# Attention scores as one fp32r product over a stack of high and low parts, in place of an fp32 product over 64 rows

## The chip, the cores and the metric

One core of one Trainium2 chip runs the whole block. The metric is the device time in microseconds of one execution. Engines: PE (TensorE, matmuls; its weight loads are listed as PEld), DVE (VectorE), ACT (ScalarE), POOL (GpSimd) and SP (SyncE, which here only issues DMAs). Each executes its own list of instructions in order and waits on semaphores.

## What is computed

A residual block for 512 tokens of width 1024: RMSNorm, one wide projection, three branches (stick-breaking attention, an mLSTM, attention into 256 memory tokens), sigmoid gates, an output projection, and then a layer of 16384 single-neuron experts. The change is in the scores of the first branch, 8 heads of 64:

```
z = jnp.einsum('bhqd,bhkd->bhqk', qi, kf) * scale            # scale = 64 ** -0.5
log_keep = jnp.where(mask, jax.nn.log_sigmoid(-z), 0.0)
suffix = lax.cumsum(log_keep, axis=3, reverse=True) - log_keep
a = jnp.where(mask, jnp.exp(jax.nn.log_sigmoid(z) + suffix), 0.0)
return jnp.einsum('bhqk,bhkd->bhqd', a, vf)
```

## The kernel before, in words

**Weights.** Nearly every product is made of "items". An item is 512 KB of weights that SP loads into one of four raw slots (`w_raw`); ACT makes its high part (`high_w`, L1337), and POOL its low part (`low_ws`, L491) or, for a few items, DVE (`low_w`, L1709). Both parts go into one of two slots (`w_r`, item number modulo 2), so the parts of item n can only be made once PE has used the slot's last item, n-2. PE multiplies in fp32r with the high part first and the low part behind it. A gate item (`gate_item(m)`, L747) is 16 products of 512 columns, an item of the memory values (L770) is 8.

**Gate items and bank 7.** The 24 gate items are strewn between the stages so that PE has work. All but one use PSUM bank 7. So `gate_item(m)` first waits on `pre_out` until DVE has copied the last one out: `take_gate(m-1)` (L1834), which stands at a fixed place of DVE's list.

**Before the attention** four items of memory values alternate with gate items 0 to 3 (items 37 to 44). On DVE the end of this stretch is `take_gate(2)`, `low_w(44)`, the copies of `mem_v` (L1847), `take_gate(3)`.

**The attention** runs over four pairs of heads, p = 0 to 3. PE's order for a pair, with m = 4 + 3p:

```
sb_scores(p); gate_item(m); sb_values(p - 1); gate_item(m + 1)
sb_suffix(2 * p); sb_suffix(2 * p + 1); gate_item(m + 2)
```

`sb_scores` (L938) multiplies keys by queries out of `projT`: fp32, 64 rows for each head, one head of the pair in rows 0 to 63 and the other in rows 64 to 127; blocks of 512, 384, 256 and 128 columns for each head. Eight mask products (L942) follow and release `z_ready`. From it ACT (Abs, Exp, Ln: L1426 to L1431) and DVE (`minus_abs`, L1917, and `keep`, L1871) make the logarithms, which both split again (`hi_part`, L1435, on ACT; `low_part`, L1887, on DVE) for `sb_suffix` (L954). DVE's list in a pair: `minus_abs`, `take_gate(m)`, `keep` twice, `low_part` twice with `take_y` (L1891) between them, `take_gate(m+1)`, in pairs 1 and 2 `split_low` (L1908 and L1911, two operations for the mLSTM, 128x512, both inputs in SBUF), `take_gate(m+2)`, and behind pairs 0 and 1 `norm_q` (L1859) and `norm_k` (L1863).

**r_all**, 1 MB of mLSTM rows broadcast to all partitions, is loaded by SP (L592) at m = 1; DVE needs it in pair 3, in `decay(0)` (L1900).

Of the kernel before, what the change touches and what calls it, by code (L numbers as in the profile page):

```python
# [133 lines left out]
def build(nc, A, out, gates_dram, pre_dram, acts_dram):  # L134
    ctx = ExitStack()
    with ctx:
# [73 lines left out]
        lk_lo = carve_r("lk_lo", 45072, 2 * CAUSAL)  # L210
        pre_stage = carve("pre_stage", 5120, 1024)

        y_ml = carve("y_ml", 40976, 2048)
# [71 lines left out]
        y_ml3 = y_ml.rearrange("p (t c) -> p t c", c=512)  # L285
        yT = [y.rearrange("p (g t) -> p g t", t=T) for y in (y_sbT, y_mlT, y_memT)]
        gate_s3 = gate_s.rearrange("p (s c) -> p s c", c=2 * T)
        conv_out = work[:, 0:1024].rearrange("p (s t) -> p s t", t=T)
# [84 lines left out]
        def mem_part(k):  # L373
# [26 lines left out]
        y_hi, y_lo, m_hi, m_lo = sem("y_hi"), sem("y_lo"), sem("m_hi"), sem("m_lo")  # L400
        if_ln = sem("if_ln")
        rows_made, thr_made, cols_turned, cols_out = sem("rows_made"), sem("thr_made"), sem("cols_turned"), sem("cols_out")
        conv_done, silu_done, x_far = sem("conv_done"), sem("silu_done"), sem("x_far")
        qk_squared, qk_rooted, qk_normed = sem("qk_squared"), sem("qk_rooted"), sem("qk_normed")
# [4 lines left out]
        ml_split_hi, ml_split_lo = sem("ml_split_hi"), sem("ml_split_lo")  # L409
        s_ready, d_ready, e_ready, e_masked, w_ready, num_done, num_out = (  # L410
            sem("s_ready"), sem("d_ready"), sem("e_ready"), sem("e_masked"), sem("w_ready"), sem("num_done"),
            sem("num_out"))
        ml_squared, ml_factors, ml_normed, mlT_done, mlT_out = (
            sem("ml_squared"), sem("ml_factors"), sem("ml_normed"), sem("mlT_done"), sem("mlT_out"))
        qkT_done, qkT_out = sem("qkT_done"), sem("qkT_out")
# [126 lines left out]
        def _(sp):  # L542
# [43 lines left out]
            for m in range(24):  # L586
                while loaded <= gate_at(m) + 4:
                    load_item(loaded, loaded % 4)
                    loaded += 1
                if m == 1:  # L590
                    sp.wait_ge(row_out, 48)
                    sp.dma_start(r_all, acts_dram[0, 0:4, :].rearrange("h t -> (h t)").partition_broadcast(P)  # L592
                                 ).then_inc(row_in, 16)
                if m == 20:
                    sp.wait_ge(s_ready, MLH)
                    sp.dma_start(xa3, A["x"].rearrange("(t p) d -> p t d", p=P)).then_inc(xa_in, 16)
                sp.wait_ge(pre_out, m + 1)
                sp.dma_start(pre_dram[m // 2, :, (m % 2) * T:(m % 2 + 1) * T],
                             pre_stage[:, (m % 2) * T:(m % 2 + 1) * T]).then_inc(pre_stored[m % 2], 16)
# [133 lines left out]
        def _(pe):  # L733
# [174 lines left out]
            def turn_rows():  # L908


                pe.wait_ge(thr_made, 1)
# [18 lines left out]

            def half(h):
                return slice(SBD * h, SBD * h + SBD)

            def sb_scores(p):
                at_least(pe, a_ready, 2 * p)
                for kt in range(TT):
                    for h in range(2):
                        pe.matmul(causal(h, kt), projT3[half(h), 4 + p, kt * P:(kt + 1) * P],  # L938
                                  projT3[half(h), p, kt * P:T], start=kt != 3, stop=False, skip_group_check=True)
                for h in range(2):  # L940
                    for kt in range(TT):
                        ins = pe.matmul(causal(h, kt)[:, 0:P], ident_bf, mask_bf, start=False, stop=False,  # L942
                                        skip_group_check=True)
                ins.then_inc(z_ready, 1)
# [362 lines left out]
        def _(act):  # L1307
# [81 lines left out]
            for n in range(7, I_IF + 3):  # L1389
# [7 lines left out]
                if n in SILU_BEHIND:  # L1397
                    silu(SILU_BEHIND[n])

            act.wait_ge(if_rows, 1)  # L1400
            link(act.activation(r_abs, r_zero, ACT.Abs, bias=bif[:, 1:2]))
            link(act.activation(r_abs, r_abs, ACT.Exp, scale=-1.0))
            high_w(I_N + 2, (I_N + 2) % 4)
            act.activation(r_abs, r_abs, ACT.Ln, bias=1.0).then_inc(if_ln, 1)
            for b in range(4):
                for j in range(4):
                    n = I_N + 4 * b + j + 2
                    if n > I_N + 2:
                        high_w(n, n % 4)
                    if (b, j) in SILU_AFTER:  # L1410
                        silu(SILU_AFTER[b, j])
            for n in range(I_KV + 2, I_G + GATES_IN_KV):
                high_w(n, n % 4)
            act.wait_ge(qk_squared, 2)
            act.activation(roots[:, S_Q:S_ML], sums[:, S_Q:S_ML], ACT.Sqrt, bias=eps_col[:, :],
                           scale=1.0 / HD).then_inc(qk_rooted, 1)
            high_w(I_G + 4, (I_G + 4) % 4)
# [35 lines left out]
            for p in range(PAIRS):  # L1453
# [4 lines left out]
                high_ws(n, n + 1)  # L1458
                exp_part(2 * p)
                exp_part(2 * p + 1)  # L1460
                high_ws(n + 2)
                if p == 0:
                    act.wait_ge(rows_made, 1)
                    act.activation(r_m, r_m, ACT.Exp, scale=-1.0).then_inc(thr_made, 1)
                if p < PAIRS - 1:
# [16 lines left out]

            act.wait_ge(ml_squared, 1)
            act.activation(roots[:, S_ML:S_H], sums[:, S_ML:S_H], ACT.Sqrt, bias=eps_col[:, :],
# [209 lines left out]
        def _(dve):  # L1694
# [62 lines left out]
            def square_keys():  # L1757
                dve.wait_ge(k_out, MT)
                link(dve.tensor_tensor(qk_squares[:, 2048:3072], mem_k, mem_k, ALU.mult))
                dve.tensor_reduce(sums[:, S_K:S_ML], qk_squares[:, 2048:3072].rearrange("p (g c) -> p g c", c=HD), AX.X,  # L1760
                                  ALU.add).then_inc(qk_squared, 1)

# [20 lines left out]
            for j in range(NT):  # L1783
                g = (j + 8) % NT
                dve.wait_ge(item_done, T_AT[j] + 1)
                if g < 4:
                    dve.scalar_tensor_tensor(out=projT3[:, g, :], in0=bank(t_bank(j)), scalar=SBD ** -0.5, in1=rstd_b,
                                             op0=ALU.mult, op1=ALU.mult).then_inc(proj_out, 1)
# [14 lines left out]
            dve.tensor_tensor(r_max, bank(0)[0:MLH, :], rstd_b[0:MLH, :], ALU.mult).then_inc(if_rows, 1)  # L1803
            dve.wait_ge(if_ln, 1)
            link(dve.tensor_scalar(r_f, r_zero, bif[:, 1:2], 0.0, ALU.add, ALU.min))
# [5 lines left out]
            link(dve.tensor_tensor_scan(r_max, r_a, r_a, 0.0, ALU.max, ALU.max))  # L1811
            dve.tensor_tensor(r_m, r_b, r_max, ALU.add).then_inc(rows_made, 1)
            natural = [sb_v3, None, ml_o3, mem_q3]
            for b in range(4):
# [11 lines left out]
                if b < 2:  # L1826
                    conv(4 + 2 * b)
                    conv(5 + 2 * b)

            def take_gate(m):  # L1830
# [6 lines left out]
            for m in range(3):  # L1837
                take_gate(m)
                low_w(I_KV + 3 + 2 * m)
                if m == 0:  # L1840
                    dve.wait_ge(n_out, 4 * TT)
                    link(dve.tensor_tensor(qk_squares[:, 0:2048], mem_q, mem_q, ALU.mult))
                    dve.tensor_reduce(sums[:, S_Q:S_K], qk_squares[:, 0:2048].rearrange("p (g c) -> p g c", c=HD), AX.X,
                                      ALU.add).then_inc(qk_squared, 1)
            dve.wait_ge(item_done, V_AT[3] + 1)
            for t in range(MT):
                dve.tensor_scalar(mem_v3[:, t, :], bank(4 + t), rstd[:, TT + t:TT + t + 1], None,  # L1847
                                  ALU.mult).then_inc(n_out, 1)
            take_gate(3)

# [4 lines left out]
            def norm_q():  # L1855
                dve.wait_ge(qk_rooted, 1)
                link(dve.reciprocal(rstd[:, S_Q:S_ML], roots[:, S_Q:S_ML]))
# [62 lines left out]
            for p in range(PAIRS):  # L1920
# [10 lines left out]
                if p == PAIRS - 1:  # L1931
                    dve.wait_ge(cols_turned, 1)
                    dve.tensor_copy(key_cols[:, :], bank(6)[:, 0:32]).then_inc(cols_out, 1)
                    decay(0)
                if 1 <= p < PAIRS - 1:
                    split_low(p - 1)
                take_gate(m + 2)
                if p == 0:
# [30 lines left out]
            for h in (0, 2):  # L1969
# [7 lines left out]
                if h == 0:  # L1977
# [5 lines left out]
            dve.tensor_reduce(sums[:, S_ML:S_H], squares.rearrange("p (g c) -> p g c", c=HD), AX.X,  # L1983
                              ALU.add).then_inc(ml_squared, 1)

# [403 lines left out]
```

## Time and profile before

| | us |
|---|---|
| median of 3 runs (1463.91 to 1464.27) | 1464.25 |
| the profiled execution, its time | 1466.18 |
| its span, first to last instruction | 1464.5 |

PE is busy for 99% of the span, DVE for 76%, ACT for 51%, POOL for 29%, at a mean granted clock of 0.999. The pairs of heads take about a twentieth of the span, from 166 us on; the experts take the second two thirds. "Busy" of PE is modelled from the starts of its instructions, so within a stretch the starts of the next block are the better ruler.

### The profile page before, as it was taken

The numbers are of one execution on the slowest core, as the hardware profiler recorded it, in microseconds if no ns is written. First come the engines' busy times: TensorE is split into PE (matmuls) and PEld (weight loads), VectorE is DVE, ScalarE is ACT, GpSimd is POOL, SyncE is SP. The second block draws the span as 40 slices with busy tenths as digits, with TensorE's granted clock in tenths as the row PEclk, the third lists the DMA queues.
The fourth block names the chain that finished last, engine by engine and source line by source line (L and its number), as shares of the span: only waits on it lengthen the run. The fifth ranks groups of instructions, "written<-read, shape, count | busy, mean of one in ns | idle before, by whom it ended". The sixth has DMA issues, their size and how long they took to land.

```text
span 1464.5 us, 22288 instructions
## 1 busy us (share of the span) xinstructions
PE 1455.2 (99%) x7466; PEld 1208.1 (82%) x7466; DVE 1107.4 (76%) x1903; ACT 747.2 (51%) x955; POOL 424.6 (29%) x200
## 2 busy tenths in 40 slices
PE   9999999999999999999999999999999999999999
PEld 8888777878788888888888888888888888888887
DVE  5977688867589999996999997346666666666665
ACT  6444677477645454554556555454444444444442
POOL 5866435436546687884000000000000000000000
PEclk9999999999999999999999999999999999999999
DMA  7544533538433666666888888988888888888883
GB/s 239 172 144 144 202 123 108 174 121 300 152 116 115 219 219 208 215 209 206 299 304 303 310 297 305 321 285 287 297 297 281 296 283 296 284 293 286 292 286 139
DMA packets 166705, 345.16 MB, mean 236 GB/s; under 512 B 13420, under 2 KB 78956, under 8 KB 164336
## 3 DMA queue, kind: packets, MB, share of 16 engines
q1 hardware_dynamic: 166640, 344.32, 69.2%
q8 instruction: 37, 0.61, 0.2%
q14 instruction: 28, 0.23, 0.0%
HBM read 268.76 MB, written 75.51 MB: 235 GB/s over the span
## 4 chain that ended last, share of the span: by engine, by line
PE 86%; DVE 10%; ACT 2%; POOL 1%; issue 0%; DMA 0%; SPq 0%; ACTq 0%; POOLq 0%
PE ps L1229 32%; PE ps L1220 25%; PE ps L747 9%; PE ps L770 6%; PE ps L1258 4%; PE ps L1089 3%; DVE top_lists L2156 1%; DVE top_lists L2149 1%; POOL u_r L538 1%; PE ps L954 1%; PE ps L735 1%; DVE top_in L2150 1%; DVE top_lists L2153 1%; DVE top_lists L2146 1%; PE ps L938 1%; PE ps L964 1%
## 5 line engine op out<-in xcount | busy, mean ns | idle before, releaser
L1220 PE MATMUL ps<-hT_r,u_r 128*128 128x512 f32 x2048 | 470.6, 391 | 0.1
L1229 PE MATMUL ps<-v_r,w_pairs 128*128 128x512 f32 x2036 | 461.7, 389 | 0.0
L1220 PEld LDWEIGHTS ps<-hT_r,u_r 128*128 128x128 f32 x2048 | 382.8, 188 | 79.7 <-POOL u_r L538 0.5
L1229 PEld LDWEIGHTS ps<-v_r,w_pairs 128*128 128x128 f32 x2036 | 382.3, 188 | 79.2
L491 POOL TENSOR_TENSOR w_r<-w_raw,w_r 128x1024 fp32r<-128x1024 f32 x85 | 217.0, 2558 | 182.5 <-ACT w_r L1337 105.0
L2295 DVE TENSOR_TENSOR v_r<-vraw,v_r 128x1024 fp32r<-128x1024 f32 x128 | 156.9, 1226 | 148.7 <-ACT v_r L1675 148.7
L1675 ACT ACTIVATE v_r<-vraw 128x1024 fp32r<-128x1024 f32 x128 | 135.7, 1061 | 253.6 <-PE ps L1229 249.0
L1622 ACT ACTIVATE act_stage<-ps 128x512 f32<-128x512 f32 x128 | 76.6, 598 | 226.5 <-PE ps L1220 226.4
L538 POOL TENSOR_TENSOR u_r<-uraw,u_r 128x1024 fp32r<-128x1024 f32 x60 | 172.9, 2892 | 46.6 <-ACT u_r L1603 46.4
L1337 ACT ACTIVATE w_r<-w_raw 128x1024 fp32r<-128x1024 f32 x95 | 100.0, 1059 | 112.2 <-PE ps L747 44.9
L1603 ACT ACTIVATE u_r<-uraw 128x1024 fp32r<-128x1024 f32 x128 | 134.9, 1054 | 15.8 <-DMA uraw<-in_u 12.9
L747 PE MATMUL ps<-xT_r,w_r 128*128 128x512 f32 x592 | 141.2, 393 | 0.0
L747 PEld LDWEIGHTS ps<-xT_r,w_r 128*128 128x128 f32 x592 | 109.8, 188 | 23.3 <-issue 0.7
L2257 DVE TENSOR_TENSOR u_r<-uraw,u_r 128x1024 fp32r<-128x1024 f32 x68 | 82.6, 1223 | 56.1 <-ACT u_r L1603 55.7
L2291 DVE TENSOR_TENSOR w_f<-act_in,g_in 128x512 f32<-128x512 f32 x128 | 87.6, 685 | 6.1 <-issue 6.1
L2298 DVE SCALAR_TENSOR_TENSOR w_pairs<-w_pairs,w_f 128x512 fp32r<-128x512 f32 x128 | 87.5, 684 | 0.0
L1677 ACT ACTIVATE w_pairs<-w_f 128x512 fp32r<-128x512 f32 x128 | 78.6, 614 | 3.8 <-DVE w_f L2291 3.8
L1645 ACT ACTIVATE stage<-ps 128x1024 f32<-128x1024 f32 x64 | 61.8, 1019 | 5.0 <-PE ps L1258 5.0
L1258 PEld LDWEIGHTS ps<-onehots 128*128 128x128 bf16 x1024 | 58.8, 97 | 4.2 <-issue 4.2
L1258 PE MATMUL ps<-onehots 128*128 128x128 bf16 x1024 | 61.6, 219 | 0.0
L770 PE MATMUL ps<-w_r,xT_r 128*128 128x512 f32 x256 | 58.2, 389 | 0.0
L770 PEld LDWEIGHTS ps<-w_r,xT_r 128*128 128x128 f32 x256 | 48.1, 188 | 10.0
(272 smaller groups left out, 1538.6 us busy)
## 6 DMA issues: line engine op xcount, KB each, us to landing
uraw<-in_u SPq DMA_DIRECT2D x128, 512.0 KB, 4.8
vraw<-in_v SPq DMA_DIRECT2D x128, 512.0 KB, 5.2
w_raw<-in_w SPq DMA_DIRECT2D x100, 512.0 KB, 3.5
acts_out<-act_stage SPq DMA_DIRECT2D x128, 256.0 KB, 2.3
gates<-stage SPq DMA_DIRECT2D x16, 2048.0 KB, 7.4
g_in<-gates SPq DMA_DIRECT2D x64, 512.0 KB, 6.4
act_in<-acts_out SPq DMA_DIRECT2D x128, 256.0 KB, 5.2
gates_pre<-pre_stage SPq DMA_DIRECT2D x24, 256.0 KB, 2.4
```

The costliest lines, as they stand in the source:

```text
L491: pool.tensor_tensor(wr4[:, n % 2, 1, :], raw3[:, n % 4, :], wr4[:, n % 2, 0, :].bitcast(F32), ALU.subtract).then_inc(w_lo_ready, 1)
L538: pool.tensor_tensor(u2[n % 4][:, 1, :], u_raw[n % 4], u2[n % 4][:, 0, :].bitcast(F32), ALU.subtract).then_inc(u_lo, 1)
L747: ins = pe.matmul(bank(b), slot_of(s)[:, w, k * P:(k + 1) * P], act[:, w, k, :], start=k + w == 0, stop=k == KD - 1 and w == 1)
L770: ins = pe.matmul(bank(b0 + t), act[:, w, 2 * j + k, t * P:(t + 1) * P], wr4[:, s, w, k * BANK:(k + 1) * BANK], start=j + k + w == 0, stop ...
L1220: ins = pe.matmul(bank(s % 2), u2[s][:, w, k * P:(k + 1) * P], hr4[:, w, k, :], start=i == 0, stop=i == 15, skip_group_check=True)
L1229: ins = pe.matmul(bank(2 * q + h), w2[:, s, w, q * P:(q + 1) * P], v2[s][:, w, h * BANK:(h + 1) * BANK], start=start and w == 0, stop=stop ...
L1258: ins = pe.matmul(ps[:, at:at + P], oh_tiles[3 * s][:, q // PAIR, :, q % PAIR], oh_tiles[3 * s + 1 + w][:, q // PAIR, :, q % PAIR], start= ...
L1337: act.activation(slot_of(n)[:, 0, :], raw3[:, q, :], ACT.Copy, scale=KEEP).then_inc(w_hi_ready, 1)
L1603: act.activation(u2[s][:, 0, :], u_raw[s], ACT.Copy, scale=KEEP).then_inc(u_hi, 1)
L1675: act.activation(v2[s][:, 0, :], vr[:, s, :], ACT.Copy, scale=KEEP).then_inc(v_hi, 1)
L2291: dve.tensor_tensor(wf[:, s % 2, :].rearrange("p (b t) -> p b t", t=BLK), ai3[:, s, :].rearrange("p (b t) -> p b t", t=BLK), g4[:, par, :, ...
L2295: dve.tensor_tensor(v2[s][:, 1, :], vr[:, s, :], v2[s][:, 0, :].bitcast(F32), ALU.subtract).then_inc(v_lo, 1)
```

## The change

A head's scaled query is now written SPREAD (128) times larger; its high part (rows 0 to 63 of a stack, or 64 to 127 for the second head of a pair) is made by ACT, and what is left, by DVE into the other 64 rows of the same stack. Keys get a stack likewise. Since the stacked query and key then have 128 rows, `sb_scores` is one fp32r product per block. There are four stacks of 64x512 pieces for a pair (query and key of two heads), so 16 more ACT operations (`stack_high`) and 16 more DVE operations (`stack_low`), and `sb_scores(p)` waits for `stack_lo` to reach 4p + 4. The stacks lie where `r_all` was, so its load moves on SP to m = 13 and behind `z_ready` of the last pair, and stack_high waits once for `rows_made`. Other semaphores are only merged to make room.

```diff
+        stack_y, stack_r, stack_x = carve_r("stack_y", 38928, 2048), carve_r("stack_r", 40976, 2048), carve_r("stack_x", 2560, 512)
+        of_y, of_r = ([s[:, i * T:(i + 1) * T] for i in range(4)] for s in (stack_y, stack_r))
+        stacks = [of_y, of_r, of_y[1:] + [stack_x], of_r]
...
-                if m == 1:
+                if m == GATES_IN_KV + 3 * (PAIRS - 1):
+                    sp.wait_ge(z_ready, PAIRS)
                     sp.wait_ge(row_out, 48)
                     sp.dma_start(r_all, acts_dram[0, 0:4, :].rearrange("h t -> (h t)").partition_broadcast(P)
...
             def sb_scores(p):
                 at_least(pe, a_ready, 2 * p)
+                pe.wait_ge(stack_lo, 4 * p + 4)
                 for kt in range(TT):
                     for h in range(2):
-                        pe.matmul(causal(h, kt), projT3[half(h), 4 + p, kt * P:(kt + 1) * P],
-                                  projT3[half(h), p, kt * P:T], start=kt != 3, stop=False, skip_group_check=True)
+                        query, key = stacks[p][2 * h:2 * h + 2]
+                        pe.matmul(causal(h, kt), key[:, kt * P:(kt + 1) * P], query[:, kt * P:T],
+                                  start=kt != 3, stop=False, skip_group_check=True)
...
+            def stack_high(p, i):
+
+                h, s = half(i // 2), stacks[p][i]
+                act.activation(s[h, :], projT3[h, i % 2 * 4 + p, :], ACT.Copy,
+                               scale=(1.0 / SPREAD, KEEP)[i % 2]).then_inc(stack_hi, 1)
...
             for n in range(I_KV + 2, I_G + GATES_IN_KV):
                 high_w(n, n % 4)
+                if n < I_KV + 6:
+                    stack_high(1, n - I_KV - 2)
...
                 exp_part(2 * p)
+                if p < 2:
+                    stack_high(p + 2, 0)
+                    stack_high(p + 2, 1)
                 exp_part(2 * p + 1)
+                if p < 2:
+                    stack_high(p + 2, 2)
+                    stack_high(p + 2, 3)
...
+            def stack_low(p, i):
+
+                h, s = half(i // 2), stacks[p][i]
+                dve.wait_ge(stack_hi, 4 * p + i + 1)
+                if i % 2:
+                    ins = dve.tensor_tensor(s[half(1 - i // 2), :], projT3[h, 4 + p, :], s[h, :].bitcast(F32), ALU.subtract)
+                else:
+                    ins = dve.scalar_tensor_tensor(out=s[half(1 - i // 2), :], in0=s[h, :].bitcast(F32), scalar=1.0 - SPREAD,
+                                                   in1=projT3[h, p, :], op0=ALU.mult, op1=ALU.add)
+                ins.then_inc(stack_lo, 1)
...
+            for i in range(2):
+                stack_low(1, i)
             dve.wait_ge(item_done, V_AT[3] + 1)
             for t in range(MT):
                 dve.tensor_scalar(mem_v3[:, t, :], bank(4 + t), rstd[:, TT + t:TT + t + 1], None,
                                   ALU.mult).then_inc(n_out, 1)
+            for i in range(2, 4):
+                stack_low(1, i)
             take_gate(3)
...
+                if p == 0:
+                    for i in range(4):
+                        stack_low(2, i)
                 if 1 <= p < PAIRS - 1:
                     split_low(p - 1)
+                    stack_low(3, 2 * p - 2)
+                    stack_low(3, 2 * p - 1)
                 take_gate(m + 2)
```

The four of pair 0 are made earlier, in the middle of the projection (behind its third block of columns).

DVE's list at the end of the memory values, before (`take_gate` is the row that writes `pre_stage`, the row of `w_r` is `low_w(44)`):

```order
L1834 TENSOR_TENSOR pre_stage<-ps,rstd_b 128x512
L1709 TENSOR_TENSOR w_r<-w_raw,w_r 128x1024
L1847 TENSOR_SCALAR mem_v<-ps,rstd 128x512 x2
L1834 TENSOR_TENSOR pre_stage<-ps,rstd_b 128x512
L1917 TENSOR_SCALAR work<-ps 128x1280
```

The same place of the changed kernel, where L1873 is `take_gate` and L1960 `minus_abs`:

```order
L1873 TENSOR_TENSOR pre_stage<-ps,rstd_b 128x512
L1734 TENSOR_TENSOR w_r<-w_raw,w_r 128x1024
L1845 SCALAR_TENSOR_TENSOR stack_r<-stack_r,projT 64x512
L1843 TENSOR_TENSOR stack_r<-projT,stack_r 64x512
L1888 TENSOR_SCALAR mem_v<-ps,rstd 128x512 x2
L1845 SCALAR_TENSOR_TENSOR stack_r<-stack_r,projT 64x512
L1843 TENSOR_TENSOR stack_r<-projT,stack_r 64x512
L1873 TENSOR_TENSOR pre_stage<-ps,rstd_b 128x512
L1960 TENSOR_SCALAR work<-ps 128x1280
```

Four operations now stand between `take_gate(2)` and `take_gate(3)`, two on either side of `mem_v`.

DVE's list at the end of pair 1, before (the last row is `minus_abs(2)`, the one above it `norm_k`):

```order
L1887 TENSOR_TENSOR lk_lo<-work,lk_hi 128x1280
L1834 TENSOR_TENSOR pre_stage<-ps,rstd_b 128x512
L1908 SCALAR_TENSOR_TENSOR projT_r<-projT_r,projT 128x512
L1911 TENSOR_TENSOR projT_r<-projT,projT_r 128x512
L1834 TENSOR_TENSOR pre_stage<-ps,rstd_b 128x512
L1863 TENSOR_TENSOR mem_k<-mem_k,rstd 128x1024
L1917 TENSOR_SCALAR work<-ps 128x1280
```

And of the changed kernel:

```order
L1930 TENSOR_TENSOR lk_lo<-work,lk_hi 128x1280
L1873 TENSOR_TENSOR pre_stage<-ps,rstd_b 128x512
L1951 SCALAR_TENSOR_TENSOR projT_r<-projT_r,projT 128x512
L1954 TENSOR_TENSOR projT_r<-projT,projT_r 128x512
L1845 SCALAR_TENSOR_TENSOR stack_r<-stack_r,projT 64x512
L1843 TENSOR_TENSOR stack_r<-projT,stack_r 64x512
L1873 TENSOR_TENSOR pre_stage<-ps,rstd_b 128x512
L1906 TENSOR_TENSOR mem_k<-mem_k,rstd 128x1024
L1960 TENSOR_SCALAR work<-ps 128x1280
```

Two operations came in ahead of the pair's last `take_gate`. At the end of pair 2 it is the same, without the row of `mem_k`.

## Rows read from the trace of the kernel before

**Rows 1.** The page: busy time by engine.

```profile
PE 1455.2 (99%) x7466; PEld 1208.1 (82%) x7466; DVE 1107.4 (76%) x1903; ACT 747.2 (51%) x955; POOL 424.6 (29%) x200
```

**Rows 2.** The chain that ended last, from 207 us: start, us, what.

```profile
207.28 2.36 PE ps L938 x16
209.64 0.55 PE ps L942 x8
210.19 3.72 PE ps L747 x16
...
224.19 3.72 PE ps L747 x16
227.90 2.36 PE ps L938 x16
...
255.41 2.51 PE ps L991 x16
```

**Rows 3.** Waits from 140 to 300 us: who waited, for whom; total, times, longest.

```profile
DVE pre_stage L1834 <- PE ps L747: 25.0, 12, 6.1
...
ACT w_r L1337 <- PE ps L747: 20.9, 10, 7.1
...
PEld ps L954 <- ACT lk_hi L1435: 0.6, 1, 0.6
...
PEld ps L954 <- DVE lk_lo L1887: 0.3, 1, 0.3
```

**Rows 4.** Timeline, 160 to 170 us: start, length, engine; times add up under "x2".

```profile
161.46 1.22 DVE L1709 TENSOR_TENSOR w_r<-w_raw,w_r 128x1024 fp32r<-128x1024 f32 x1
162.71 1.41 DVE L1847 TENSOR_SCALAR mem_v<-ps,rstd 128x512 f32<-128x512 f32 x2
163.04 1.06 ACT L1337 ACTIVATE w_r<-w_raw 128x1024 fp32r<-128x1024 f32 x1 [1.27 <-DMA w_raw<-in_w]
164.26 4.71 POOL L491 TENSOR_TENSOR w_r<-w_raw,w_r 128x1024 fp32r<-128x1024 f32 x2 [4.29 <-ACT w_r L1337]
166.26 2.43 PE L938 MATMUL ps<-projT 64*128 64x512 f32 x16
169.05 7.54 PE L747 MATMUL ps<-xT_r,w_r 128*128 128x512 f32 x32
```

**Rows 5.** Timeline, 200 to 211 us, DVE and POOL.

```profile
200.73 6.15 POOL L491 TENSOR_TENSOR w_r<-w_raw,w_r 128x1024 fp32r<-128x1024 f32 x2 [11.63 <-ACT w_r L1337]
202.32 2.30 DVE L1908 SCALAR_TENSOR_TENSOR projT_r<-projT_r,projT 128x512 fp32r<-128x512 f32 x1
204.54 2.89 DVE L1911 TENSOR_TENSOR projT_r<-projT,projT_r 128x512 fp32r<-128x512 f32 x1
207.43 2.35 POOL L491 TENSOR_TENSOR w_r<-w_raw,w_r 128x1024 fp32r<-128x1024 f32 x1 [0.55 <-PE ps L747]
207.95 2.91 DVE L1863 TENSOR_TENSOR mem_k<-mem_k,rstd 128x1024 f32<-128x1024 f32 x1
```

**Rows 6.** Timeline, 222 to 231 us, DVE and POOL.

```profile
225.15 2.89 DVE L1911 TENSOR_TENSOR projT_r<-projT,projT_r 128x512 fp32r<-128x512 f32 x1
228.05 2.35 POOL L491 TENSOR_TENSOR w_r<-w_raw,w_r 128x1024 fp32r<-128x1024 f32 x1 [0.56 <-PE ps L747]
```

**Rows 7.** Timeline, 268 to 271 us, DVE while POOL is idle.

```profile
268.90 0.68 DVE L1908 SCALAR_TENSOR_TENSOR projT_r<-projT_r,projT 128x512 fp32r<-128x512 f32 x1
269.49 0.69 DVE L1911 TENSOR_TENSOR projT_r<-projT,projT_r 128x512 fp32r<-128x512 f32 x1
```

**Rows 8.** DMA issues: KB each, us to landing.

```profile
r_all<-acts_out SPq DMA_DIRECT2D x1, 1024.0 KB, 8.1
```

**Rows 9.** Stretches: length; PE, PEld, DVE, ACT, POOL busy; granted clock, DMA share, GB/s.

```profile
5.00:8.00 3.00, 1.95 (x17) 1.71 (x17) 0.97 (x3) 0.11 (x1) 0.00 (x0) 1.00 0.91 316
8.00:12.00 4.00, 3.42 (x15) 1.90 (x12) 3.74 (x8) 4.00 (x10) 3.16 (x6) 1.00 1.03 416
12.00:16.00 4.00, 4.00 (x21) 4.00 (x22) 2.79 (x6) 1.34 (x4) 0.98 (x3) 0.58 1.02 411
```

More of the change, by code:

```diff
@@ L286, in build, with half @@
         yT = [y.rearrange("p (g t) -> p g t", t=T) for y in (y_sbT, y_mlT, y_memT)]
+        of_y, of_r = ([s[:, i * T:(i + 1) * T] for i in range(4)] for s in (stack_y, stack_r))
+        stacks = [of_y, of_r, of_y[1:] + [stack_x], of_r]
+        def half(h):
+            return slice(SBD * h, SBD * h + SBD)
         gate_s3 = gate_s.rearrange("p (s c) -> p s c", c=2 * T)
@@ L400, in build @@
         y_hi, y_lo, m_hi, m_lo = sem("y_hi"), sem("y_lo"), sem("m_hi"), sem("m_lo")
-        if_ln = sem("if_ln")
-        rows_made, thr_made, cols_turned, cols_out = sem("rows_made"), sem("thr_made"), sem("cols_turned"), sem("cols_out")
+        rows_made, if_made, cols_turned, cols_out = sem("rows_made"), sem("if_made"), sem("cols_turned"), sem("cols_out")
         conv_done, silu_done, x_far = sem("conv_done"), sem("silu_done"), sem("x_far")
-        qk_squared, qk_rooted, qk_normed = sem("qk_squared"), sem("qk_rooted"), sem("qk_normed")
+        qk_normed = sem("qk_normed")
         z_ready, ln_ready, keep_ready = sem("z_ready"), sem("ln_ready"), sem("keep_ready")
@@ L409, in build @@
         ml_split_hi, ml_split_lo = sem("ml_split_hi"), sem("ml_split_lo")
+        stack_hi, stack_lo = sem("stack_hi"), sem("stack_lo")
         s_ready, d_ready, e_ready, e_masked, w_ready, num_done, num_out = (
@@ L412, in build @@
             sem("num_out"))
-        ml_squared, ml_factors, ml_normed, mlT_done, mlT_out = (
-            sem("ml_squared"), sem("ml_factors"), sem("ml_normed"), sem("mlT_done"), sem("mlT_out"))
+        ml_factors, ml_normed, mlT_done, mlT_out = (
+            sem("ml_factors"), sem("ml_normed"), sem("mlT_done"), sem("mlT_out"))
         qkT_done, qkT_out = sem("qkT_done"), sem("qkT_out")
@@ L908, in turn_rows @@
             def turn_rows():
-                pe.wait_ge(thr_made, 1)
+                pe.wait_ge(if_made, 2)
                 pe.wait_ge(y_out, PAIRS - 1)
@@ L927, in part @@
                 return buf[:, CAUSAL_AT[kt] + (q0 - kt) * P:CAUSAL_AT[kt] + (q1 - kt) * P]
-            def half(h):
-                return slice(SBD * h, SBD * h + SBD)
             def sb_scores(p):
                 at_least(pe, a_ready, 2 * p)
+                pe.wait_ge(stack_lo, 4 * p + 4)
                 for kt in range(TT):
                     for h in range(2):
-                        pe.matmul(causal(h, kt), projT3[half(h), 4 + p, kt * P:(kt + 1) * P],
-                                  projT3[half(h), p, kt * P:T], start=kt != 3, stop=False, skip_group_check=True)
+                        query, key = stacks[p][2 * h:2 * h + 2]
+                        pe.matmul(causal(h, kt), key[:, kt * P:(kt + 1) * P], query[:, kt * P:T],
+                                  start=kt != 3, stop=False, skip_group_check=True)
                 for h in range(2):
@@ L1403, in _ @@
             high_w(I_N + 2, (I_N + 2) % 4)
-            act.activation(r_abs, r_abs, ACT.Ln, bias=1.0).then_inc(if_ln, 1)
+            act.activation(r_abs, r_abs, ACT.Ln, bias=1.0).then_inc(if_made, 1)
             for b in range(4):
@@ L1411, in _ @@
                         silu(SILU_AFTER[b, j])
+                    if (b, j) == (1, 3):
+                        act.wait_ge(proj_out, NT)
+                    if b == 2:
+                        stack_high(0, j)
+            act.wait_ge(rows_made, 1)
             for n in range(I_KV + 2, I_G + GATES_IN_KV):
                 high_w(n, n % 4)
-            act.wait_ge(qk_squared, 2)
+                if n < I_KV + 6:
+                    stack_high(1, n - I_KV - 2)
+            act.wait_ge(squared, 3)
             act.activation(roots[:, S_Q:S_ML], sums[:, S_Q:S_ML], ACT.Sqrt, bias=eps_col[:, :],
-                           scale=1.0 / HD).then_inc(qk_rooted, 1)
+                           scale=1.0 / HD).then_inc(rooted, 1)
             high_w(I_G + 4, (I_G + 4) % 4)
@@ L1463, in _ @@
                     act.wait_ge(rows_made, 1)
-                    act.activation(r_m, r_m, ACT.Exp, scale=-1.0).then_inc(thr_made, 1)
+                    act.activation(r_m, r_m, ACT.Exp, scale=-1.0).then_inc(if_made, 1)
                 if p < PAIRS - 1:
@@ L1481, in _ @@
             act.activation(mem_kT, bank(4, 2), ACT.Copy, scale=cols[:, C_KG:C_KG + 1]).then_inc(qkT_out, 1)
-            act.wait_ge(ml_squared, 1)
+            act.wait_ge(squared, 4)
             act.activation(roots[:, S_ML:S_H], sums[:, S_ML:S_H], ACT.Sqrt, bias=eps_col[:, :],
@@ L1760, in square_keys @@
                 dve.tensor_reduce(sums[:, S_K:S_ML], qk_squares[:, 2048:3072].rearrange("p (g c) -> p g c", c=HD), AX.X,
-                                  ALU.add).then_inc(qk_squared, 1)
+                                  ALU.add).then_inc(squared, 1)
             dve.wait_ge(row_in, 16)
@@ L1786, in _ @@
                 if g < 4:
-                    dve.scalar_tensor_tensor(out=projT3[:, g, :], in0=bank(t_bank(j)), scalar=SBD ** -0.5, in1=rstd_b,
+                    dve.scalar_tensor_tensor(out=projT3[:, g, :], in0=bank(t_bank(j)), scalar=SBD ** -0.5 * SPREAD, in1=rstd_b,
                                              op0=ALU.mult, op1=ALU.mult).then_inc(proj_out, 1)
@@ L1803, in _ @@
             dve.tensor_tensor(r_max, bank(0)[0:MLH, :], rstd_b[0:MLH, :], ALU.mult).then_inc(if_rows, 1)
-            dve.wait_ge(if_ln, 1)
+            dve.wait_ge(if_made, 1)
             link(dve.tensor_scalar(r_f, r_zero, bif[:, 1:2], 0.0, ALU.add, ALU.min))
@@ L1828, in _ @@
                     conv(5 + 2 * b)
+                elif b == 2:
+                    for i in range(4):
+                        stack_low(0, i)
             def take_gate(m):
@@ L1843, in _ @@
                     dve.tensor_reduce(sums[:, S_Q:S_K], qk_squares[:, 0:2048].rearrange("p (g c) -> p g c", c=HD), AX.X,
-                                      ALU.add).then_inc(qk_squared, 1)
+                                      ALU.add).then_inc(squared, 1)
+            for i in range(2):
+                stack_low(1, i)
             dve.wait_ge(item_done, V_AT[3] + 1)
@@ L1855, in norm_q @@
             def norm_q():
-                dve.wait_ge(qk_rooted, 1)
+                dve.wait_ge(rooted, 3)
                 link(dve.reciprocal(rstd[:, S_Q:S_ML], roots[:, S_Q:S_ML]))
@@ L1934, in _ @@
                     decay(0)
+                if p == 0:
+                    for i in range(4):
+                        stack_low(2, i)
                 if 1 <= p < PAIRS - 1:
                     split_low(p - 1)
+                    stack_low(3, 2 * p - 2)
+                    stack_low(3, 2 * p - 1)
                 take_gate(m + 2)
@@ L1983, in _ @@
             dve.tensor_reduce(sums[:, S_ML:S_H], squares.rearrange("p (g c) -> p g c", c=HD), AX.X,
-                              ALU.add).then_inc(ml_squared, 1)
+                              ALU.add).then_inc(squared, 1)
             def gate_ml():
```

## The prediction

> **What bounds the kernel now.** I read the page first: PE is busy for 99% of the span [rows 1]. Then the chain of work that ended last, in time: through the pairs of heads it runs block by block down PE's list, with no break [rows 2]. So a microsecond less on PE in a pair is a microsecond less in the end, and so is one in which PE stands still, since all that follows hangs on the pairs through data or through PE's order. The list of waits shows how little PE waits there: 0.6 and 0.3 us, both in pair 0's suffix [rows 3]. The other engines have idle time, but idle time is no free place: `take_gate` holds bank 7, and it stands behind everything that DVE was given before it.
>
> **What the products give.** A pair's score block takes 2.36 us [rows 2], 2560 columns for its two heads. The nearest fp32r block over 128 rows with the same four widths is that of the mLSTM scores (L991): 16 products, 5120 columns, 2.51 us [rows 2]. The new block is half of it, 1.26. The gain is 1.1 us a pair, 4.4 us in all. Bounds: no gain, if the stacked block took 2.36 as now, and 4.8 if it ran at the pace of a gate item (8192 columns in 3.72 [rows 2], so 1.16).
>
> The row of 2.36 also says what is given up. The Trainium skill says that true fp32 takes four passes through the array (FP8 and Floating Point Precision, "TensorE Precision Notes"), and that tiles of 64 rows work independently of one another (TensorEngine Tiling (Array Packing), "Key Properties"). By the first rule alone, an estimate, the old block would take 2560 x 4 / 2.4 GHz = 4.27 us and the gain would be 3.0 a pair, 12 in all; with the second, which speaks against the change, 2.13 and 0.9 a pair, 3.5 in all. The row decides between them, near the second.
>
> **ACT's part.** 16 copies of about 0.6 us. From 140 us on ACT waited for PE ten times before a weight part, 20.9 us in all [rows 3], and the copies fit there. In pairs 0 and 1 they put `exp_part` and the next weight parts back by under 1 us; the low part of the next gate item is made by POOL at 207.43, 4.4 us before PE wants it (second half of the item that starts at 210.19). Cost: nothing.
>
> **r_all.** It is issued when the last pair's `z_ready` comes and takes 8.1 us [rows 8]. DVE needs it behind that pair's suffix, some 13 us after `z_ready` (209.64 + 0.55 to 224.19 is 14 in the pair shown [rows 2]). Hidden, with 5 us to spare; were it not, `decay(0)` would wait on DVE, not PE. SP stands at that wait only when its next instruction would wait for later work anyway.
>
> **DVE's part, the cost.** A small operation with two SBUF inputs takes 0.68 us, and 0.60 from start to start, when POOL is idle [rows 7]. The same two take 2.30 and 2.89 beside POOL, and POOL's pair of low parts takes 6.15 instead of 4.71 [rows 5, 4]. 2.89 is 2.3 of a POOL low part plus 0.6; they take turns: the first waits for POOL's first, then POOL's second runs, then the second gets its turn. `mem_k`, at 207.95, ends only 1.1 after POOL's 207.43 + 2.35 [rows 5]. So I count each new `stack_low` as 0.6 plus what is left of a POOL low part that got in first (2.35 [rows 5]), and I follow the queues at the four places.
>
> *End of the memory values.* `low_w(44)` ends at 162.7 [rows 4], and `stack_low(1,0)` runs to 163.3. POOL's first low part came at 164.26, since ACT waited 1.27 us for weights [rows 4]; the load ahead of them in the queue was r_all, 8.1 us from issue to landing [rows 8], now gone, so ACT starts at some 161.8, and POOL asks at 162.9 and gets its turn at 163.3. `stack_low(1,1)` comes behind it, 165.6 to 166.2; `mem_v` takes 1.4, to 167.6. POOL's second low part (its slot is free when PE is done with gate item 3, 166.3 [rows 4]) runs 166.4 to 168.8, then the last two `stack_low` to 170.0, and `take_gate(3)` to 170.6. The masks take 0.43 more (169.05 - 166.26 - 2.36 [rows 4, 2]), so PE ends scores and masks at 166.3 + 1.26 + 0.43 = 168.0 and `gate_item(4)` waits for bank 7: **2.6 us**. Had r_all not mattered, it is 2.3 to 2.7. On the other side the waits of [rows 3] go, since PE comes later than the logarithms: -0.7 (between 0.6 and 0.9). With the 1.1 gained pair 0 ends 0.8 us later than before.
>
> *Pair 0.* Four `stack_low` between `take_gate(5)` and `take_gate(6)`, where DVE had 6.1 us idle [rows 3]. They and POOL's second low part fill it; `take_gate(6)` ends as the next masks do. The chain of `norm_q` and `minus_abs(1)` then comes some 0.7 us late against PE, which leaves 0.1 to 0.3 us of wait in pair 1's suffix. **0.1.**
>
> *End of pair 1.* PE has got back 1.1 - 0.1 and is 0.2 ahead of before, so the rows can be read nearly as they stand. L1911 ended at 207.43, and POOL's next low part began then [rows 5]. Now the new chain puts DVE 0.5 later, and `stack_low(3,0)` waits behind that low part: 207.9 + 2.35 + 0.6 + 0.6 = 211.5, `take_gate(9)` 212.1. PE is done with masks at 207.1 + 1.7 = 208.8. **3.3 us** at `gate_item(10)`.
>
> *End of pair 2.* The same, PE and DVE now 2.0 late (3.3 - 0.2 - 1.1): L1911 ends at 228.04 and POOL's low part at 230.4 [rows 6], two `stack_low` to 231.6, plus 2.0 is 233.6. Here the scores themselves need both; PE is there at 227.9 + 2.0 = 229.9. **3.7 us** before `sb_scores(3)`.
>
> Sum of the queues: 2.6 - 0.7 + 0.1 + 3.3 + 3.7 = 9.0 lost, 4.4 gained: **+4.6 us**. Bounds: if the new operations never waited for POOL, DVE would have them done in its idle time and -4.4 is left; with 0.68 each from start to start, the eleven of 0.08 that lie on the way and the waits of the suffix behind them make it some +6.
>
> The trace has no operation over 64 partitions beside POOL, so the nearest row is the same operation over 128 [rows 5]. A rule that bears on it is in the Trainium skill (SBUF — State Buffer, "Who interferes with whom"): a DVE instruction with two SBUF inputs and a GpSimd instruction that reads SBUF exclude each other for the whole instruction, and no number of partitions is named. By it the sum is +4.6; without it, -4.4.
>
> **The clock.** PE's longest stand in the pairs before is 0.6 us [rows 3]. Now it would be 2.6, 3.3 and 3.7. The trace has one fall of the granted clock: 0.58 from 12 to 16 us, which is mostly the lower level, after two stretches in which PE was busy for 1.95 of 3 and 3.42 of 4 us [rows 9]. It loses 4 x 0.42 = 1.7 us of full speed, and in the pairs PE is the bound. Up to three falls, 5.1 us; none is the other bound. I take two: **+3.4**.
>
> **The sum**, against the profiled execution: 1466.2 + 4.6 + 3.4 = 1474.2. That execution lies 1.9 above the median of the runs, so for the median 1464.25 + 8.0 = 1472.3.
>
> **The rivals.**
> - *The queues, but no fall of the clock, 1468.9.* For it: each stand is a single one with dense work on either side. Against it: each is longer than the 1.05 and 0.58 us that PE stood ahead of the one fall [rows 9]. 0.2.
> - *The saving arrives, 1459.9, faster.* One mechanism: the 64-partition operations don't take turns with POOL, or DVE gets both of a pair through before POOL asks. It decides at the end of pairs 1 and 2: if the last `stack_low` is done by the time that PE's masks are (208.8), nothing is left of 3.3 and 3.7. For it: nothing but the missing row; POOL's own start depends on PE, and 0.6 us earlier for DVE changes only who goes first, not the sum. 0.15.
> - *Part of the stands only, 1463 to 1467.* One or two of the three shrink, POOL's low part falling beside the pair. 0.15, a third of it within the bound of no change.
> - *More, over 1476.* Three falls and 0.68 an operation. 0.05.
> - The forecast, queues and one to three falls, 1470.5 to 1476: 0.45.
>
> **How the numbers follow.** 0.2% is 2.9 us, about what tells a time of this kernel from no change. Slower is the forecast, its no-fall rival and the rest above 1467.2: 0.45 + 0.2 + 0.05 + 0.05 = 0.75. Same takes 0.08 of the partial case; faster 0.15 and the remainder, 0.17. The range leaves out the case of the full saving and the worst: 1463 to 1476. The likeliest case's own range is 1470.5 to 1476.
>
> **What would show it.** Score blocks of 1.26 us from first score to first mask. New DVE rows of 64x512 that take 0.6 or about 2.9. A wait of PE before L747 at about 168 us and about 208.8 released by DVE's `pre_stage`, and one before the last scores released by `stack_r`. Windows at half clock behind them. I am wrong if those DVE rows all take 0.7 beside busy POOL, or if PE's waits come from ACT.

## The result, and the profile after

The changed kernel takes 1474.2 us (median of 6, 1472.15 to 1475.81) against 1464.8 us before (median of 6): 0.63% slower, ratio 1.0063, 95% interval 1.0053 to 1.0074. Each group of experiments below has runs of the kernel before of its own (medians 1464.9 to 1465.3), and "before" is those. The prediction was 1472.3 us, slower with 0.75.

The profiled execution is the slowest of the six, 1475.81 us with a span of 1473.7. Waits of the changed kernel from 140 to 300 us (who waited, for whom: total, times, longest); before, PE's only ones in the pairs were those of [rows 3]:

```profile
PE ps L754 <- DVE pre_stage L1873: 5.3, 2, 3.0
...
PE ps L944 <- DVE stack_r L1843: 3.7, 1, 3.7
...
DVE stack_y L1845 <- ACT stack_y L1409: 1.5, 1, 1.5
...
PEld ps L960 <- ACT lk_hi L1454: 0.3, 1, 0.3
```

Two waits of gate items for `take_gate`, one of scores for the last `stack_low`, and pair 0's suffix no longer waits, apart from 0.3. PE's timeline of the changed kernel (start, length; L944 are the scores, L948 the masks, L754 the gate items), which answers to [rows 2] and the PE rows of [rows 4]:

```profile
164.71 1.38 PE L944 MATMUL ps<-stack_y 128*128 128x512 f32 x8
165.94 0.62 PE L948 MATMUL ps<-mask_bf,ident_bf 128*128 128x128 bf16 x8
168.91 9.17 PE L754 MATMUL ps<-xT_r,w_r 128*128 128x512 f32 x32 [2.35 <-DVE pre_stage L1873]
187.39 1.38 PE L944 MATMUL ps<-stack_r 128*128 128x512 f32 x8
...
208.13 0.62 PE L948 MATMUL ps<-mask_bf,ident_bf 128*128 128x128 bf16 x8
211.73 6.65 PE L754 MATMUL ps<-xT_r,w_r 128*128 128x512 f32 x16 [2.97 <-DVE pre_stage L1873]
218.31 2.37 PE L970 MATMUL ps<-work,sb_v 128*64 128x512 f32 x16
...
236.12 2.58 PE L944 MATMUL ps<-stack_r 128*128 128x512 f32 x8 [3.71 <-DVE stack_r L1843]
```

A score block lasts 1.23 us from first product to first mask (165.94 - 164.71), was 2.36. But gate item 10 lasts 6.58 (218.31 - 211.73) and was 3.85 in the same ruler, two gate items 9.17 where they were 7.54, and the last scores 2.58 where those of the other pairs are 1.38: PE at half its clock. The granted clock is 0.50 in three stretches, 169.8 to 173.2, 210.8 to 217.6 and 234.7 to 241.5 us, the first 0.9 us after PE's wait has ended, the others from 1.0 and 1.4 us before the end of theirs; two of them in windows drawn by the blocks (PEclk is the column before the DMA share):

```profile
212.00:219.00 7.00, 7.00 (x20) 4.99 (x22) 2.79 (x3) 3.17 (x3) 0.00 (x0) 0.60 0.34 112
...
236.10:245.00 8.90, 8.88 (x36) 7.06 (x38) 2.78 (x4) 5.29 (x5) 0.00 (x0) 0.70 0.59 208
```

DVE and POOL at the end of pair 1 in the changed kernel, which answer to [rows 5]:

```profile
202.46 2.30 DVE L1951 SCALAR_TENSOR_TENSOR projT_r<-projT_r,projT 128x512 fp32r<-128x512 f32 x1
204.69 2.89 DVE L1954 TENSOR_TENSOR projT_r<-projT,projT_r 128x512 fp32r<-128x512 f32 x1
207.61 2.73 DVE L1845 SCALAR_TENSOR_TENSOR stack_r<-stack_r,projT 64x512 fp32r<-64x512 f32 x1
210.27 0.68 DVE L1843 TENSOR_TENSOR stack_r<-projT,stack_r 64x512 fp32r<-64x512 f32 x1
210.98 0.69 DVE L1873 TENSOR_TENSOR pre_stage<-ps,rstd_b 128x512 f32<-128x512 f32 x1
```

```profile
200.88 6.16 POOL L497 TENSOR_TENSOR w_r<-w_raw,w_r 128x1024 fp32r<-128x1024 f32 x2 [10.85 <-ACT w_r L1343]
207.37 2.43 POOL L497 TENSOR_TENSOR w_r<-w_raw,w_r 128x1024 fp32r<-128x1024 f32 x1 [0.33 <-ACT w_r L1343]
```

The first `stack_low` on 64 partitions stands behind POOL's operation until it ends at 209.80, the second beside idle POOL takes 0.68, and `take_gate(9)` ends at 211.67, 3.1 us after the masks (208.13 + 0.43). At the other two places it is the second `stack_low` of the pair that stands behind POOL longest:

```profile
165.28 2.85 DVE L1843 TENSOR_TENSOR stack_r<-projT,stack_r 64x512 fp32r<-64x512 f32 x1
...
233.15 2.83 DVE L1843 TENSOR_TENSOR stack_r<-projT,stack_r 64x512 fp32r<-64x512 f32 x1
```

**The pairs added up.** From first scores to first scores (164.71, 187.39, 206.90, 236.12, then the mLSTM scores at 264.98) the pairs last 22.7, 19.5, 29.2 and 28.9 us, and lasted 20.3, 20.6, 20.6 and 27.4. That is 11.3 more in this execution, and its span is 9.2 longer. Of the 2.0 between, 0.5 lies in the output projection, whose 192 products take 44.5 us in the profiled execution of before and 44.0 in this one; why is open. The other 1.5 lie at the start, where the profiled execution of before had its fall of the clock (second row) and this one had none (first row):

```profile
8.00:16.00 8.00, 7.41 (x49) 5.89 (x48) 7.30 (x14) 6.87 (x16) 5.30 (x11) 1.00 1.03 416
```

```profile
8.00:16.00 8.00, 7.42 (x35) 5.90 (x33) 6.53 (x12) 5.34 (x13) 4.13 (x8) 0.79 1.02 413
```

So a fall at the start is a cost that comes and goes from execution to execution, and the profiled run of before (1466.18, median 1464.25) was one that had it. The time less the span is 1.7 us before and 2.1 in the changed kernel and in every one below that makes the stacks: 0.4 us of the loss lie outside the instructions that the spans cover.

### The profile page after: what moved, and what is told of

Its sections match the earlier page's. It is cut to its first block, busy times and chain, and to the rows that moved or that the text cites. A ratio compares the mean times of both kernels' runs of the same rounds, so it can differ in the third digit from the quotient of the medians.

```text
span 1473.7 us, 22262 instructions
## 1 busy us (share of the span) xinstructions
PE 1456.0 (99%) x7434; PEld 1211.2 (82%) x7434; DVE 1125.2 (76%) x1919; ACT 756.3 (51%) x971; POOL 427.1 (29%) x200
## 4 chain that ended last, share of the span: by engine, by line
PE 82%; DVE 13%; ACT 1%; POOL 1%; issue 1%; DMA 0%; SPq 0%; ACTq 0%; POOLq 0%; DVEq 0%
PE ps L1235 31%; PE ps L1226 25%; PE ps L754 8%; PE ps L777 6%; PE ps L1264 4%; PE ps L1095 3%; DVE top_lists L2204 1%; DVE top_lists L2197 1%; POOL u_r L544 1%; PE ps L742 1%; DVE top_in L2198 1%; DVE top_lists L2201 1%; DVE top_lists L2194 1%; PE ps L1008 1%; DVE work L1914 1%
## 5 line engine op out<-in xcount | busy, mean ns | idle before, releaser
L754 PE MATMUL ps<-xT_r,w_r 128*128 128x512 f32 x592 | 146.6, 404 | 5.3 <-DVE pre_stage L1873 5.3
L754 PEld LDWEIGHTS ps<-xT_r,w_r 128*128 128x128 f32 x592 | 113.7, 195 | 30.4 <-DVE pre_stage L1873 5.7
```

The costliest lines, as they stand in the source:

```text
L754: ins = pe.matmul(bank(b), slot_of(s)[:, w, k * P:(k + 1) * P], act[:, w, k, :], start=k + w == 0, stop=k == KD - 1 and w == 1)
```

## The experiments

Theory: three places in DVE's list where `stack_low` stands behind POOL, with which it takes turns, PE standing there, and a low clock after it. Rivals: too much work for DVE or ACT wherever it stands; a low clock that falls into the waits and costs nothing; products that are not faster where it counts.

**Only the products.** The wait for `stack_lo` and the bodies of both stack functions go:

```diff
-                pe.wait_ge(stack_lo, 4 * p + 4)
...
-                        query, key = stacks[p][2 * h:2 * h + 2]
+                        query, key = xr4[:, 0, p, :], xr4[:, 0, 4 + p, :]
```

> The changed kernel without its 32 stack operations and without the wait for them; the scores multiply blocks of xT_r, the normalised input that lies in SBUF in fp32r over 128 rows, so they are fp32r products of the same shapes on other numbers. It has what the change gives and none of what it costs. Theory: 4.4 us below the kernel before, 1460; score blocks of 1.23 us instead of 2.36. Rival, the shorter blocks give nothing because ACT's and DVE's chain from z_ready bounds the pairs: 0 to 1 us below.

1459.5 us (5 runs), ratio 0.9961 (0.9948 to 0.9974), 5.3 below before. Its four score blocks start at 164.85, 183.96, 203.47 and 222.85, so pairs 0 to 2 are 1.2, 1.1 and 1.2 us shorter: the gain is real and arrives. Pair 3 is 1.1 shorter as well (26.3 us to the mLSTM scores, 27.4 before), so the pairs give 4.7 of it, and the 0.5 of the output projection is in this kernel too (44.0 us in place of 44.5). What makes that 0.5 isn't shown; this kernel also has r_all's move and the merged semaphores.

**Only the stacks.** The scores again as before, with the query scaled as before, behind the wait:

```diff
-                        query, key = stacks[p][2 * h:2 * h + 2]
...
+                        pe.matmul(causal(h, kt), projT3[half(h), 4 + p, kt * P:(kt + 1) * P],
+                                  projT3[half(h), p, kt * P:T], start=kt != 3, stop=False, skip_group_check=True)
```

> The changed kernel with the old scores, fp32 over 64 rows of projT, behind the same wait for stack_lo; all 32 stack operations stay. It has what the change costs and none of what it gives. Theory, from the queues: the waits before gate items 4 and 10 are each 1.1 us shorter, as the scores cover them, the one before the last scores stays: 2.6 - 1.1 + 3.3 - 1.1 + 3.7 less 0.7 is 6.7 us, and one fall of the clock or two: 8 to 11 us above the kernel before, 1473 to 1475, so that the gain of the products is nearly lost inside the waits. Rival, the costs add simply, what the change costs being 9.4 + 4.4: 1478.

1474.1 us (6 runs), ratio 1.0062 (1.0050 to 1.0074): as long as the changed kernel. PE's waits in it:

```profile
PE ps L943 <- DVE stack_r L1842: 3.8, 1, 3.8
...
PE ps L754 <- DVE pre_stage L1872: 1.5, 1, 1.5
...
PE ps L943 <- DVE mem_v L1887: 1.4, 1, 1.4
```

6.7 us, as much as expected, but made up otherwise: before gate item 4 there is no wait where 1.5 was expected, before gate item 10 it is 1.5 and not 2.2, and the first scores stand for `mem_v` (below), which I had not expected. With the stacks where they are, faster products are worth nothing: PE comes sooner to where it waits, and waits longer (9.6 us in the changed kernel), and the mean granted clock is lower, 0.994 to 0.998 against 0.996 to 0.999 here.

**POOL steps back.** Three waits more, no work less:

```diff
-            low_ws(I_G + GATES_IN_KV, 14)
+            low_ws(I_G + GATES_IN_KV, 1)
+            pool.wait_ge(stack_lo, 8)
+            low_ws(I_G + GATES_IN_KV + 1, 6)
+            pool.wait_ge(stack_lo, 14)
+            low_ws(I_G + GATES_IN_KV + 7, 3)
+            pool.wait_ge(stack_lo, 16)
+            low_ws(I_G + GATES_IN_KV + 10, 4)
```

> The changed kernel with three waits more on POOL: its low parts of items 46, 52 and 55 wait until the stack_low that stand at that place are done (stack_lo 8, 14 and 16). No engine has less work, only the order at the port is turned round. Theory (two inputs in SBUF and POOL exclude each other): stack_low takes 0.7 us everywhere there, the waits before gate items 4 and 10 and before the last scores fall by up to 2.3 us each, of which the late low part of item 52 gives back 0.5 to 1 us in the middle of gate item 10; with less low clock 6 to 9 us below the changed kernel, 1465 to 1468. Rival, it is DVE's own amount of work that is late: no change or slower, since POOL now starts later.

1465.4 us (12 runs), ratio 1.0004 (0.9995 to 1.0012): 8.8 below the changed kernel. DVE, POOL and PE at the end of pair 1:

```profile
206.53 0.69 DVE L1851 SCALAR_TENSOR_TENSOR stack_r<-stack_r,projT 64x512 fp32r<-64x512 f32 x1
207.13 0.68 DVE L1849 TENSOR_TENSOR stack_r<-projT,stack_r 64x512 fp32r<-64x512 f32 x1
207.85 0.69 DVE L1879 TENSOR_TENSOR pre_stage<-ps,rstd_b 128x512 f32<-128x512 f32 x1
207.89 2.39 POOL L497 TENSOR_TENSOR w_r<-w_raw,w_r 128x1024 fp32r<-128x1024 f32 x1 [1.95 <-DVE stack_r L1849]
...
208.59 0.73 PE L760 MATMUL ps<-xT_r,w_r 128*128 128x512 f32 x2 [0.92 <-DVE pre_stage L1879]
```

The row of 2.73 is 0.69, and PE's waits at the ends of pairs 1 and 2 are 0.9 and 1.7 in place of 3.0 and 3.7. In the same execution a `stack_low` that stands beside POOL still takes 2.89 (182.42 us, pair 0). An engine that does its work later makes the kernel faster; the rival of DVE's own amount of work is out, since DVE does the same work here.

**PE kept busy.** 36 products into a bank nobody uses, inside the waits:

```diff
+            def fill(count):
+                for i in range(count):
+                    pe.matmul(bank(6), xr4[:, 0, 0, 0:P], xr4[:, 0, 0, :], start=True, stop=True)
...
+                if p == PAIRS - 1:
+                    fill(15)
                 sb_scores(p)
+                if p in (0, 2):
+                    fill((10, 0, 11)[p])
```

> The changed kernel with 36 more products of 512 columns into the free bank 6, put where PE stands: 10 before gate item 4, 11 before gate item 10, 15 before the last scores, 2.2, 2.4 and 3.3 us of work inside waits of 2.5, 3.0 and 3.7 to 4.1 us. They leave the queues as they are and keep PE busy. If the clock is a cost of its own, its mean is 0.999 again and the time is 3 to 5 us below the changed kernel, 1469 to 1471, in every execution, so the spread of 3.7 us between executions goes too. Rival, the low clock falls into the waits and costs nothing: no change, or slower by what does not fit.

1470.2 us (6 runs, 1469.46 to 1471.22), ratio 1.0036 (1.0024 to 1.0049): 4.0 below the changed kernel with 36 products more. The executions lie within 1.8 us of one another, those of the changed kernel within 3.7. The granted clock stays whole:

```profile
160.00:180.00 20.00, 19.97 (x103) 16.52 (x102) 17.26 (x16) 14.81 (x15) 6.04 (x3) 1.00 0.53 181
205.00:240.00 35.00, 34.12 (x186) 26.43 (x184) 29.65 (x25) 23.02 (x22) 11.73 (x5) 1.00 0.38 131
```

So the clock is a cost of its own, some 4 us in the median. What is left over before, 5.2, is near the 4.4 of the queues (summed below) and the 0.4 outside the spans.

**The places apart.** The first move, in the list of DVE:

```diff
-            for i in range(2, 4):
-                stack_low(1, i)
             take_gate(3)
...
                 minus_abs(p)
+                if p == 0:
+                    for i in range(2, 4):
+                        stack_low(1, i)
                 take_gate(m)
```

> Only the first of the two moves: stack_low(1, 2) and (1, 3) behind minus_abs(0). Theory: the wait before gate item 4 (2.5 us) goes, and with it the fall of the clock behind it (1.6 us lost from 170 to 180 us in the profiled execution); the 0.6 to 0.9 us of waits in pair 0's suffix come back. 3 to 3.5 us below the changed kernel, about 1471. Rival, one wait taken away only moves to the next: no change.

1470.3 us (5 runs), ratio 1.0036 (1.0022 to 1.0049): 3.9 below the changed kernel. The second move:

```diff
                 minus_abs(p)
+                if p == PAIRS - 1:
+                    split_low(0)
+                    split_low(1)
...
                 if 1 <= p < PAIRS - 1:
-                    split_low(p - 1)
                     stack_low(3, 2 * p - 2)
```

> Only the second move: split_low(0) and (1) behind minus_abs(3). Theory: the waits of 3.0 and 3.7 us at the ends of pairs 1 and 2 go, and the low clock behind them (3.4 and 3.5 us lost in the profiled execution, part of it while PE stood): 9 to 12 us below the changed kernel, 1462 to 1465. Rival, the lost time lies with ACT, whose list is unchanged: no change.

1462.6 us (11 runs), ratio 0.9983 (0.9974 to 0.9992): 11.6 below, the greater part as expected. In its profiled execution PE still waits before gate item 4, and the clock stays whole (1.00 from 165 to 240 us):

```profile
PE ps L754 <- DVE pre_stage L1873: 2.5, 1, 2.5
```

So a wait of that length brings a fall in one execution and none in another.

**Both moves**, each instruction of the changed kernel still there:

> The changed kernel with DVE's list reordered and nothing else: stack_low(1, 2) and (1, 3) behind minus_abs(0), where DVE waits for gate item 4, and split_low(0) and (1) behind minus_abs(3), so that between the last two take_gate of pairs 1 and 2 only two small operations stand, as before the change. Queues and clock (my theory): no take_gate and no scores are late, no wait of PE over 0.5 us, no fall of the clock in the pairs, and the gain of the products is left: 4.4 us below the kernel before, 1460 to 1461. Rival, the added work itself is too much for DVE and ACT wherever it stands: at or above the kernel before, 1465 or more.

1461.8 us (11 runs, 1459.88 to 1463.19), ratio 0.9977 (0.9968 to 0.9986): faster than before, by 3.2 and not by 4.4, and 12.4 below the changed kernel. The moves don't add up (3.9 and 11.6 alone): the first is worth only 0.8 once the second is made, so the medians don't say what each place costs. Of the missing 1.2, 0.4 lie outside the span (above). Its profiled execution is one of the quick ones (1460.48), and in it PE waits for `stack_r` for 0.3 only. The profiled executions of the first move alone, of the stacks alone and of POOL's waits all have a row that this one lacks; in that of the first move it is

```profile
PE ps L944 <- DVE mem_v L1888: 1.4, 1, 1.4
```

with DVE and POOL in the same execution:

```profile
161.34 2.89 DVE L1843 TENSOR_TENSOR stack_r<-projT,stack_r 64x512 fp32r<-64x512 f32 x1
164.26 1.41 DVE L1888 TENSOR_SCALAR mem_v<-ps,rstd 128x512 f32<-128x512 f32 x2
```

```profile
161.07 2.60 POOL L497 TENSOR_TENSOR w_r<-w_raw,w_r 128x1024 fp32r<-128x1024 f32 x1 [3.10 <-ACT w_r L1343]
```

POOL began at 161.07, before `stack_low(1, 1)` at 161.34. In the changed kernel's profiled execution DVE was 0.3 us ahead (`stack_low(1, 1)` at 161.85, POOL from 162.18) and the scores did not wait. What differs is how long ACT, which makes the high part ahead of POOL's low part, waits for the raw weights; in the changed kernel:

```profile
160.96 1.06 ACT L1343 ACTIVATE w_r<-w_raw 128x1024 fp32r<-128x1024 f32 x1 [0.65 <-DMA w_raw<-in_w]
```

In the four profiled executions in which DVE was first (the changed kernel, PE kept busy, the second move alone, both moves) ACT waited 0.65 to 1.06 us for them, in the four in which POOL was (the first move alone, only the stacks, POOL's waits, and both moves once more, below) 0 to 0.17. The same kernel, both moves, is on either side, so the order changes from execution to execution.

**Values first.** Both moves, and `stack_low(1, 0)` and `(1, 1)` behind `minus_abs(0)` too, with both moves once more beside it:

```diff
-            for i in range(2):
-                stack_low(1, i)
...
-                    for i in range(2, 4):
+                    for i in range(4):
                         stack_low(1, i)
```

> The kernel with both moves, and stack_low(1, 0) and (1, 1) too behind minus_abs(0), so that nothing stands before mem_v, for which the first scores wait (n_out). In the profiled executions of the first move alone and of POOL's three waits, POOL got the port ahead of stack_low(1, 1), mem_v came late, and the scores stood for 1.4 us; in those of the changed kernel and of both moves DVE was first and they did not. If that is what spreads the times of both moves (1459.9 to 1463.2), the new median is at their lower end, 1460 to 1460.5, and no execution is above 1462. Rival, the spread is the clock at the start alone, as in the kernel before: the same median, 1461.8, and the same spread.

> The kernel with both moves once more, on the same chip as the one beside it: 1461 to 1462, 1 to 1.5 us above it by the first account, level with it by the rival.

1460.7 us (7 runs, 1459.88 to 1461.97), ratio 0.9972 (0.9961 to 0.9984), and 1461.9 us (11 runs, 1459.53 to 1464.49), ratio 0.9976 (0.9967 to 0.9985). The medians lie 1.2 apart as expected, no execution with values first is above 1462, and the profiled one of its neighbour has the 1.4 us wait for `mem_v`. It also has the fall of the clock at the start (0.79 from 8 to 16 us), so the spread of both moves has two sources, and the rival is right about one of them. The intervals against before overlap, so that it is better than both moves is likely, not settled; that it beats before by 0.28% is. It is 4.6 below before, so with values first the 4.4 of the products arrive whole.

## Why the prediction was right

- **The products**: 1.23 us a block (said 1.26), 1.13 gained a pair. Right. The row of 2.36, not the four passes alone, gave the size.
- **DVE and POOL taking turns**: the part in which rows and the rule of the Trainium skill met (SBUF — State Buffer, "Who interferes with whom"). Right, and it holds for 64 partitions: 2.73 and 2.83 us beside POOL, 0.68 without. That POOL's turn is the cause is shown by POOL's three waits.
- **End of the memory values**: said a wait of 2.6 before gate item 4, measured 2.54 (168.91 - 165.94 - 0.43), though not by the way I took. I had POOL ahead of `stack_low(1, 1)`, and `mem_v` at 167.6. In the profiled execution DVE was first and `stack_low(1, 3)`, at 2.85, brought the delay. Where POOL is first, as I had it, I missed that `sb_scores(0)` waits for `mem_v`: PE stands before the scores. That the size came out all the same is partly luck. The order that I had worked out can be priced only by an estimate from the run with only the stacks, where POOL was first: scores from 165.79 with 1.23 and 0.43 us would end at 167.45, and gate item 4 began at 168.85, so 1.4 there and 1.4 before the scores, 2.8 in all. No execution of the changed kernel with POOL first was profiled.
- **Pair 0**: said 0.1, none measured: pair 1 is 1.1 us shorter, all of the gain.
- **Ends of pairs 1 and 2**: said 3.3 and 3.7, measured 3.17 (211.73 - 208.56) and 3.87 (from 232.25, 3.72 after the last gate item began at 228.53, to 236.12). Right in place, releaser and size; in pair 2 it is the second `stack_low` that waits for POOL and not the first, at the same price.
- **The queues' sum**: said +4.6. In the profiled execution 2.54 - 0.69 + 3.17 + 3.87 - 4 x 1.13 is +4.4, the 0.69 being what pair 0 gets back in the suffix (22.68 - 20.33 is 2.54 - 1.13 - 0.69 + 1.63 of clock). With the clock's 6.9 that is the 11.3 of the pairs; less 2.0 at the start and in the output projection, and with 0.4 outside the span, it is the 9.6 between the two profiled times. The prediction has neither the 0.5 of the output projection nor the 0.4 outside the span; they nearly cancel.
- **The clock**: said two falls, 3.4 us. In the profiled execution it took 1.6, 2.7 and 2.6 us after the three waits, 6.9 in all, and in the median some 4 by the filled kernel. The mechanism was right; as a size for this execution it was too small. All three waits had a fall behind them, and the two later falls lasted 6.8 us and not the 3.4 of the one before, so that each cost some 2.7 and not 1.7. The mean granted clock of the six executions goes from 0.994 (1475.8 and 1475.2 us) to 0.998 (1473.0 and 1472.2), and the times with it.
- **ACT and r_all at nothing**: no wait of PE is ACT's beyond 0.3; DVE's 1.5 us for `stack_y` in pair 0 reaches no wait of PE; and `decay` starts at 253.6 without a wait for r_all, which is issued at 239.6 and lands 5.6 us later. Right.
- Of the rivals, the one without a fall (1468.9) is what the filled kernel comes near to, 1470.2. Of the 1.9 us between the forecast of 1472.3 and the 1474.2 measured, 0.5 is the median of before, which six runs put at 1464.8 where I had 1464.25 from three, and some 0.6 is the clock; the rest is not split.

## What to carry to other kernels

Before an operation is put where an engine "has time", ask what stands behind it in that engine's list and who waits for that; here 32 operations of 0.6 us made a kernel 9.4 us slower that would have been some 5 faster, and moving six of DVE's instructions brought 12.4 us back. Where the operations of two engines take turns, as DVE's and POOL's here, count a small operation at the length of the other's large one, and keep such operations out of stretches where both are due. A wait of TensorE of some 3 us is to be priced with the half clock that may follow: here 4 us in the median, 6.9 in the slowest execution, behind 9.6 us of such waits. The length of a wait alone doesn't tell: one of 2.5 had no fall behind it (the second move alone), one of 1.7 had one (POOL's waits, 0.50 from 229.8 to 233.1 us).

## What the runs showed that I had not expected

The order in which DVE and POOL take their turns changes from execution to execution: half a microsecond or more in the arrival of raw weights went with whether the first scores stood for 1.4 us. And making one engine later (POOL, which stood idle for 2 to 3.5 us at three places) made the kernel 8.8 us faster.
